# Second attention: each query pair in one weight block with the rope columns twice, keys projected first; the last expert group in smaller pieces with its end on two engines

## The chip, the cores and the metric

One NeuronCore of one Trainium2 chip runs the whole program in one launch. The time is device microseconds of that core, the median over several runs of the same kernel. The kernel before takes 1916.61 us (three runs, 1916.44 to 1920.51). All arithmetic is float32 or its rounded parts, batch 1, 256 tokens (two tiles of 128 partitions), model width 1024.

## What is computed

A small network of two blocks and a third one behind it: FoX attention, SwiGLU, MLA attention (the second attention), SwiGLU, final norm; then a token mixer (stick-breaking attention and gated delta rule), cross attention over 256 memory rows, and PEER, a layer that reads 16 expert rows for each token and each of 8 heads. The parts that matter here:

```python
def rope(x, positions):                       # x1, x2: the halves of 32 columns
    out = concat([x1 * cos - x2 * sin, x1 * sin + x2 * cos])

def mla_attention(xn, positions, k, v, w_dq, cq_norm, w_uq, w_o):   # 16 heads
    c_q = rmsnorm(xn @ w_dq, cq_norm)                     # 768 wide
    q = (c_q @ w_uq).reshape(B, S, 16, 64 + 32)
    q = concat([q[..., :64], rope(q[..., 64:], positions)])
    # k of a head: 64 columns c_kv @ w_uk, and 32 rope columns shared by all heads
    o = causal_block_attention(q, k, v, 1 / sqrt(96))
    return o @ w_o

def peer(xn, w_pq, subkeys, peer_u, peer_v):
    # for each of 8 heads: the 16 best of 16384 experts for each token, and then
    act = gelu(einsum('thkd,td->thk', peer_u[eb], xb)) * gate
    out = einsum('thk,thkd->td', act, peer_v[eb])

# and at the very end: h + out, root-mean-square norm with g_final
```

## The kernel before

Each engine has a program of its own, in order, and they meet at semaphores. `Tally` counts the waits, also in loops. SP issues nearly all loads; weights go into four single slots of SBUF, `SLOT[0..3]`. `fill(s, ...)` waits until slot s is used up and then issues; TensorE frees a slot with `release(s)`, which queues the signal, and `first(m)` hangs it on the next matmul that takes one, so a slot is free when a matmul *behind* its last reader has ended. PSUM has eight banks; `take` and `evacuated` make TensorE wait until VectorE ("v") or ScalarE ("a") has read a bank.

**Second attention.** The 16 heads run as 8 pairs. For a pair TensorE does `mla_proj` (line 853): queries of head 0 and head 1, each 96 rows by 256 columns over six chunks of 128 (slot 0, 576 KB), then the 64 key rows of each head over two chunks (slot 1, 128 KB), each head in a group of its own, then a product of the copied queries `QRAW` with the matrix `rot`, which turns the rope halves. Each matmul of float32 is two passes. ScalarE copies queries and keys out (`mla_copy`, 1544). VectorE's `rotate` (2128) multiplies the turned queries by sines and the queries by cosines, and adds: three operations. The shared rope rows of the keys are computed once and stand in rows 64 to 96 of `KT` for both heads. `mla_scores` (TensorE 874, VectorE 2136) gives the scores with a contraction over 96 rows, ScalarE the exponentials (`two_probs`), and `attend` (654) turns them (`flip`), multiplies them with the values (`mix_values`) and turns the result (`turn`). The order in the loop is scores of pair i+1, projection of pair i+2, attention of pair i+1. SP issues the query fill and then the key fill of a pair (`qk`, 367).

**ffn** (both). Behind the last block VectorE adds the residual in four halves, ScalarE squares each half (1475), VectorE does mean and reciprocal, and ScalarE the square root (`root`, 1399).

**Expert layer.** For each head and token tile ("unit", 16 in all) GpSimd gathers 16 rows of 8 KB a token (u and v, `gather`, 1790) into a ring. VectorE takes the dot product of a row with the token (`dots`, 2559); after four of them ScalarE does Gelu, VectorE the gate weight, ScalarE four diagonal matrices (`diagonals`, 1721), and TensorE multiplies them with the v rows into four PSUM banks that add up over all heads (`mix_v`, 1354), four passes a row. After the last unit of a tile a product with zeros closes its two banks. `finish(t)` (2590) on VectorE adds both banks to `H`, squares each half, sums, takes mean and reciprocal, has ScalarE take the root, and multiplies the whole tile with it and the gain; SP then writes the tile out (469).

## Time and profile before

| | us |
|---|---|
| median of 3 runs | 1916.61 |
| profiled execution | 1915.84 |
| its span | 1913.6 |
| TensorE busy (matmul) | 1693.1 (88%) |
| VectorE busy | 1036.7 (54%) |
| ScalarE busy | 530.0 (28%) |
| GpSimd busy | 348.0 (18%) |
| mean granted TensorE clock | 0.956 of 2.4 GHz |

The profile is of one execution. Its span is the time between the first and the last instruction; 2.2 us of the execution's time lie outside. PE is TensorE, PEld its weight loads, DVE is VectorE, ACT ScalarE, POOL GpSimd, SP SyncE, and SPq the transfers that SP issues. A timeline row names start, length, engine, line of the kernel, operation with what it writes and reads, how many instructions it merges, and in brackets the engine's idle time before it with what ended it. A row "x32" of 7.22 us is 32 passes of TensorE. The second attention's loop stands from about 431 to 534 us, the two ffn end near 370 and 766, the expert layer begins near 1240, and its last unit at about 1875.

### The profile page before, as it was taken

The numbers are of one execution on the slowest core, as the hardware profiler recorded it, in microseconds if no ns is written. First come the engines' busy times: TensorE is split into PE (matmuls) and PEld (weight loads), VectorE is DVE, ScalarE is ACT, GpSimd is POOL, SyncE is SP. The second block draws the span as 40 slices with busy tenths as digits, with TensorE's granted clock in tenths as the row PEclk, the third lists the DMA queues.
The fourth block names the chain that finished last, engine by engine and source line by source line (L and its number), as shares of the span: only waits on it lengthen the run. The fifth ranks groups of instructions, "written<-read, shape, count | busy, mean of one in ns | idle before, by whom it ended". The sixth has DMA issues, their size and how long they took to land.

```text
span 1913.6 us, 22345 instructions
## 1 busy us (share of the span) xinstructions
PE 1693.1 (88%) x7695; PEld 1174.5 (61%) x7695; DVE 1036.7 (54%) x2431; ACT 530.0 (28%) x1067; POOL 348.0 (18%) x296
## 2 busy tenths in 40 slices
PE   6798999889989999799999999987888877888876
PEld 5687999856649999587565586543443433444332
DVE  5454555433435555345735201587676777766764
ACT  2353444312324443243211001122221212212211
POOL 2550000000000000000000000244434444443440
PEclk9899999999999999899999999989999989899988
DMA  7342655501336665143232532299999999999995
GB/s 240 114 111 89 197 173 179 166 16 54 115 91 198 197 179 161 36 136 115 100 121 76 209 133 80 106 419 421 421 422 421 421 421 421 422 420 422 421 421 241
DMA packets 205557, 435.63 MB, mean 228 GB/s; under 512 B 11584, under 2 KB 136896, under 8 KB 171584
## 3 DMA queue, kind: packets, MB, share of 16 engines
q0 software_dynamic: 36864, 268.45, 33.8%
q1 hardware_dynamic: 168640, 166.45, 27.3%
q8 instruction: 36, 0.59, 0.1%
q14 instruction: 17, 0.14, 0.0%
HBM read 433.79 MB, written 1.05 MB: 227 GB/s over the span
## 4 chain that ended last, share of the span: by engine, by line
PE 68%; DMA 20%; DVE 7%; issue 3%; ACT 2%; POOL 1%; SPq 0%; DVEq 0%; POOLq 0%
PE ps L505 36%; DMA OT<-in_peer_uv,IX 17%; PE ps L1359 10%; PE ps L691 6%; PE ps L1149 3%; PE ps L1006 3%; PE ps L1019 3%; PE ps L536 1%; DMA SLOT<-in_fox_w_in 1%; PE ps L511 1%; DVE SLOT L2563 1%; DVE SLOT_R L1927 1%; PE ps L1098 1%; DVE AR L2241 1%; PE ps L595 1%
## 5 line engine op out<-in xcount | busy, mean ns | idle before, releaser
L1797 POOL DMA_INDIRECT SLOT<-in_peer_uv,IX x128 | 138.3, 1080 | 1345.7 <-DVE IX L2557 1097.8
L1359 PE MATMUL ps<-SLOT,AR 128*128 128x512 f32 x512 | 268.0, 680 | 102.4 <-ACT AR L1725 102.4
L1359 PEld LDWEIGHTS ps<-SLOT,AR 128*128 128x128 f32 x512 | 109.6, 219 | 254.5 <-issue 132.2
L505 PE MATMUL ps<-ARH 128*128 128x256 f32 x2112 | 257.0, 283 | 5.1 <-DVE SM L1958 5.1
L505 PEld LDWEIGHTS ps<-ARH 128*128 128x128 f32 x2112 | 256.2, 192 | 7.0 <-issue 5.5
L2563 DVE SCALAR_TENSOR_TENSOR SLOT<-SLOT,V 128x1024 f32<-128x1024 f32 x128 | 153.4, 1224 | 77.7 <-DMA SLOT<-in_peer_uv,IX 75.6
L1927 DVE TENSOR_TENSOR ARH<-SLOT,ARH 128x2048 fp32r<-128x2048 f32 (+1 forms) x88 | 154.1, 1755 | 47.9 <-ACT ARH L1437 31.2
L1359 PE MATMUL ps<-AR 128*128 128x512 f32 x320 | 142.5, 594 | 8.1 <-ACT AR L1725 8.1
L691 PE MATMUL ps<-ARH 128*128 128x512 f32 x528 | 123.9, 390 | 0.0
L1719 ACT ACTIVATE AR<-AR 128x4 f32<-128x4 f32 x64 | 13.1, 205 | 380.9 <-DVE SLOT L2563 180.2
L691 PEld LDWEIGHTS ps<-ARH 128*128 128x128 f32 x528 | 97.7, 188 | 19.4
L1359 PEld LDWEIGHTS ps<-AR 128*128 128x128 f32 x320 | 59.7, 190 | 80.4 <-issue 64.1
L2563 DVE SCALAR_TENSOR_TENSOR AR<-AR,V 128x1024 f32<-128x1024 f32 x80 | 95.3, 1222 | 24.6 <-DMA AR<-in_peer_uv,IX 24.6
L1797 POOL DMA_INDIRECT AR<-in_peer_uv,IX x80 | 91.7, 1146 | 76.3 <-PE ps L1359 70.8
L505 PE MATMUL ps<-XT,SLOT 128*128 128x256 f32 (+1 forms) x464 | 102.1, 380 | 0.8 <-issue 0.8
L505 PEld LDWEIGHTS ps<-XT,SLOT 128*128 128x128 f32 (+1 forms) x464 | 87.2, 189 | 13.9 <-issue 1.5
L505 PE MATMUL ps<-AR,SLOT 128*96 128x256 f32 (+2 forms) x384 | 87.5, 386 | 1.2 <-issue 1.2
L1725 ACT ACTIVATE AR<-CT,AR 128x128 f32<-128x128 f32 x256 | 81.8, 390 | 17.6 <-DVE AR L2577 17.6
L1941 DVE TENSOR_TENSOR AR<-AR,ps 128x256 f32<-128x256 f32 x44 | 18.5, 421 | 125.3 <-ACT AR L1447 125.3
L1437 ACT CAST ARH<-SLOT 128x2048 fp32r<-128x2048 f32 x44 | 83.4, 1899 | 0.0
L505 PEld LDWEIGHTS ps<-AR,SLOT 128*96 128x96 f32 (+2 forms) x384 | 64.4, 170 | 22.6 <-issue 5.1
L505 PE MATMUL ps<-XT 128*128 128x256 f32 (+1 forms) x288 | 60.8, 367 | 6.7 <-DMA XT<-in_w_pq_by_head 5.6
(396 smaller groups left out, 2488.0 us busy)
## 6 DMA issues: line engine op xcount, KB each, us to landing
SLOT<-in_w_gate SPq DMA_DIRECT2D x44, 512.0 KB, 4.0
SLOT<-in_w_up SPq DMA_DIRECT2D x44, 512.0 KB, 5.3
SLOT<-in_w_down SPq DMA_DIRECT2D x44, 512.0 KB, 5.6
SLOT<-in_w_in SPq DMA_DIRECT2D x9, 2048.0 KB, 8.1
SLOT<-in_fox_w_in SPq DMA_DIRECT2D x16, 512.0 KB, 5.3
SLOT<-in_w_ckv SPq DMA_DIRECT2D x4, 2048.0 KB, 8.1
XT<-in_w_pq_by_head SPq DMA_DIRECT2D x8, 1024.0 KB
SLOT<-in_mla_w_uq SPq DMA_DIRECT2D x8, 576.0 KB
```

What stands on the lines that cost most here:

```text
L505: m = pe.matmul(outp, l, r, start=(n_ == 0), stop=(n_ == len(pairs) - 1))
L511: return pe.transpose(outp, src, IDENT)
L691: m = pe.matmul(ps[:, o_, :], l_, r_, start=(start and b == 0 and n_ == 0), stop=(stop and b == 1 and n_ == 2))
L1006: m = pe.matmul(ps[:, b, :], cols(XT, t, k), slot(s_, KC, 512)[:, k, :], start=(k == 0), stop=(k == KC - 1))
L1019: m = pe.matmul(ps[:, b, h * P:(h + 1) * P], l(h), r(h), start=True, stop=True)
L1149: m = pe.matmul(ps[:, b, :], cols(X, t, k), w[:, k, :], start=(k == 0), stop=(k == KC - 1))
L1359: m = pe.matmul(ps[:, 2 * t + c, :], DIAG[:, j, :], v_row(j)[:, c * 512:(c + 1) * 512], start=False, stop=False)
L1437: act.copy(WGU[:, b, 0].rearrange("p g k n -> p (g k n)"), SLOT[b][:, 0:2 * KC * P]).then_inc(sem("high_ready"), 1)
L1725: act.activation(DIAG[:, j, :], IDENT, ACT.Copy, scale=AV[:, t, j:j + 1]).then_inc(sem("diag_ready"), 1)
L1797: pool.indirect_dma_start(PAIR[j], None, pairs, bass.IndirectOffsetOnAxis(IX[:, t, j:j + 1], 0)).then_inc(gathered[j], 16)
L1927: return TT(out_, x, high.bitcast(F32), ALU.subtract)
L2563: m = STT(u_row(j), u_row(j), 1.0, V[:, t, :], ALU.mult, ALU.mult, accum_out=DOT[:, t, j:j + 1])
```

## The change

*Weights, on the host.* `w_uq` is laid out by pair in 256 columns instead of 192: for head 0 64 plain columns, 32 rope columns, the same 32 with halves swapped; for head 1 32 rope, 32 swapped, 64 plain. A row of the new tensor is 2048 values (8192 bytes; before, 1536 values). `w_krope` holds the 32 rope columns four times. Constants: `rot` for 128 rows, frequencies for all rows, a `sign` column.

*Second attention.* The queries come out of the projection as 128 rows a head that already hold both forms; one multiplication by a table `TABQ` (ones, cosines, signed sines) replaces copy, rotation product and the three operations. Scores contract over 128 rows. Keys of both heads come from one group of 128 rows, projected ahead of the queries; ScalarE copies each head's 64 rows. The signal that frees the key slot hangs on the queries, the one that frees the query slot on the next transpose, or, for the first pair, on the first score matmul. SP still issues the query fill first; it is 768 KB now. The table costs VectorE two memsets, two copies and two multiplications where two copies were.

*ffn.* ScalarE does a one-element Sqrt behind its last Silu, ahead of the squares.

*Last unit and end.* The rows of the last unit of tile 1 go in groups of 4, 4, 4, 2, 1, 1. The last row's two matmuls close the banks themselves. The end of tile 1: VectorE adds a half, ScalarE squares the first half and the second half's last 256 columns, VectorE squares the other 256; ScalarE writes the first half of the output from a product with the gain that VectorE made ahead, VectorE the second; each half has a transfer of 256 KB. Tile 0 ends as before, with its two additions ahead of its squares. Several semaphores of the token mixer are merged into two (`heads_ready`, `decays_ready`), signalled and waited for in the same order.

```diff
@@ host
-    arrays["in_w_krope"] = np.concatenate([np.zeros((D, 64), np.float32), np.asarray(inputs["w_kv_a"])[:, KVR:]], 1)
+    arrays["in_w_krope"] = np.ascontiguousarray(np.tile(np.asarray(inputs["w_kv_a"])[:, KVR:], (1, P // ROPE)))
+    by_pair = [nope[:, :, 0], rope[:, :, 0], swapped[:, :, 0], rope[:, :, 1], swapped[:, :, 1], nope[:, :, 1]]
@@ sync
-            qk(rows(w_uq, 0, 192), w_uk[:, :, 0:P])
+            qk(rows(w_uq, 0, 2 * P), w_uk[:, :, 0:P])
             with T.loop("mla", PAIRS - 1) as i:
-                qk(dyn(w_uq, i * 192 + 192, 192), w_uk[:, :, ds(i * P + P, P)])
+                qk(dyn(w_uq, i * 2 * P + 2 * P, 2 * P), w_uk[:, :, ds(i * P + P, P)])
...
+            sp.wait_ge(sem("result"), 2)
+            sp.dma_start(y[:, 1, 0:512], H[:, 1, 0:512]).then_inc(sem("out_done"), 16)
+            sp.wait_ge(sem("last_result"), 1)
+            sp.dma_start(y[:, 1, 512:], H[:, 1, 512:]).then_inc(sem("out_done"), 16)
@@ tensor
             def mla_proj():
+                pe.wait_ge(here[1], T.next(here[1], 16))
+                take(6)
+                group(ps[:, 6, 0:S], ((slot(1, 2, P)[:, k, :], CKT[:, k, :]) for k in range(2))).then_inc(full["a"][6], 1)
+                release(1)
+                T.add(free["a"][6])
                 pe.wait_ge(here[0], T.next(here[0], 16))
                 take(0)
                 for hh in range(2):
-                    m = group(ps[0:96, 0, hh * S:(hh + 1) * S], ((slot(0, 6, 192)[:, k, 96 * hh:96 * hh + 96], CQT[:, k, :]) for k in range(6)))
+                    m = group(ps[:, 0, hh * S:(hh + 1) * S], ((slot(0, 6, 2 * P)[:, k, P * hh:P * hh + P], CQT[:, k, :]) for k in range(6)))
                 release(0)
...
-                for hh in range(2):
-                    m = group(ps[0:64, 6, hh * S:(hh + 1) * S], ((slot(1, 2, P)[:, k, 64 * hh:64 * hh + 64], CKT[:, k, :]) for k in range(2)))
-                release(1)
...
-                first(pe.matmul(ps[0:96, 7, 0:S], const("rot", 96), QRAW[0:96, 0, :], start=True, stop=True))
-                pe.matmul(ps[0:96, 7, S:2 * S], const("rot", 96), QRAW[0:96, 1, :], start=True, stop=True).then_inc(full["v"][7], 1)
...
             def mla_scores(i):
-                evacuated(6, 7)
+                evacuated(0, 6)
                 for hh in range(2):
                     take(1 + hh)
-                    pe.matmul(ps[:, 1 + hh, 0:P], QT[0:96, hh, 0:P], KT[0:96, hh, 0:P], start=True, stop=True)
+                    first(pe.matmul(ps[:, 1 + hh, 0:P], QT[:, hh, 0:P], KT[:, hh, 0:P], start=True, stop=True))
...
+            mix_v(1, range(TOPK - 1))
+            mix_v(1, range(TOPK - 1, TOPK), closing=True)
@@ scalar, ffn
                 for b in range(2):
                     gated(b)
+                act.activation(ASCR[:, 0:1], CT[:, 0:1], ACT.Sqrt)
@@ scalar, mla_copy
-                act.wait_ge(full["a"][0], T.next(full["a"][0]))
-                act.copy(QRAW[0:96, :, :], view(ps[0:96, 0, :], 2, S)).then_inc(free["a"][0], 1)
                 act.wait_ge(full["a"][6], T.next(full["a"][6]))
-                act.copy(KT[0:64, :, :], view(ps[0:64, 6, :], 2, S)).then_inc(free["a"][6], 1)
+                act.copy(KT[0:64, 0, :], ps[0:64, 6, 0:S])
+                act.copy(KT[64:P, 1, :], ps[64:P, 6, 0:S]).then_inc(free["a"][6], 1)
@@ scalar, end
-            weigh(1, between=lambda: root_of(0))
-            root_of(1)
+            weigh(1, between=lambda: root_of(0), groups=LAST)
+            act.activation(ASCR[:, 0:1], CT[:, 0:1], ACT.Sqrt)
+            for c, part in ((0, slice(0, 512)), (1, slice(256, 512))):
+                act.wait_ge(sem("grown"), T.next(sem("grown")))
+                m = act.activation(square(1, c)[:, part], H[:, 1, c * 512:(c + 1) * 512][:, part], ACT.Square, accum_out=SS[:, 2 * c:2 * c + 1])
+            m.then_inc(sem("squared"), 1)
...
+            act.activation(H[:, 1, 0:512], V[:, 0, 0:512], ACT.Copy, scale=RS[:, 1:2]).then_inc(sem("result"), 1)
@@ vector
             def rotate():
-                dve.wait_ge(full["v"][7], T.next(full["v"][7]))
-                TT(ANG[R96, 0:2, :], view(ps[R96, 7, :], 2, S), SIN[R96, :, :], ALU.mult)
-                TT(ANG[R96, 2:4, :], QRAW[R96, :, :], COS[R96, :, :], ALU.mult).then_inc(chain, 1)
-                dve.wait_ge(chain, T.next(chain))
-                TT(QT[R96, :, :], ANG[R96, 0:2, :], ANG[R96, 2:4, :], ALU.add).then_inc(free["v"][7], 1)
-                T.add(free["v"][7])
+                dve.wait_ge(full["v"][0], T.next(full["v"][0]))
+                TT(QT[:], view(ps[:, 0, :], 2, S), TABQ, ALU.mult).then_inc(free["v"][0], 1)
+                T.add(free["v"][0])
...
+            def finish_last():
+                half = grown_half(1, 0)
+                signal("grown")
+                TT(V[:, 0, 0:512], half, ROWG[:, 0:512], ALU.mult).then_inc(sem("gained_half"), 1)
+                half = grown_half(1, 1)
+                signal("grown")
+                STT(square(1, 1)[:, 0:256], half[:, 0:256], 1.0, half[:, 0:256], ALU.mult, ALU.mult, accum_out=SS[:, 1:2]).then_inc(chain, 1)
+                dve.wait_ge(chain, T.next(chain))
+                dve.wait_ge(sem("squared"), T.next(sem("squared")))
+                dve.tensor_reduce(SS[:, 3:4], SS[:, 0:3], AX, ALU.add).then_inc(chain, 1)
...
+                STT(half, half, RS[:, 1:2], ROWG[:, 512:], ALU.mult, ALU.mult).then_inc(sem("last_result"), 1)
```

## Rows read from the trace of the kernel before

**Rows 1.** The page's part 4, the chain that ended last, by engine.
```profile
PE 68%; DMA 20%; DVE 7%; issue 3%; ACT 2%; POOL 1%; SPq 0%; DVEq 0%; POOLq 0%
```

**Rows 2.** Timeline, one head pair: start us, us, engine, line, operation, idle before.
```profile
469.60 7.22 PE L505 MATMUL ps<-AR,SLOT 128*96 128x256 f32 x32
...
474.98 0.58 ACT L1546 COPY AR<-ps 96x512 f32<-96x512 f32 x1 [2.38 <-PE ps L505]
...
475.73 0.37 SPq L355 DMA_DIRECT2D SLOT<-in_mla_w_uq  x1
...
476.74 0.67 PE L870 MATMUL ps<-AR,CT 96*96 96x256 f32 x2
...
477.68 0.82 PE L511 MATMUL ps<-CT,AR 128*128 128x128 f32 x6
...
477.70 0.37 SPq L355 DMA_DIRECT2D SLOT<-in_w_uk  x1
...
479.16 0.88 PE L505 MATMUL ps<-V,AR 128*128 x6 [0.66 <-ACT AR L1423]
...
481.07 0.46 PE L878 MATMUL ps<-AR 96*128 96x128 f32 x2 [0.19 <-issue]
...
482.45 7.22 PE L505 MATMUL ps<-AR,SLOT 128*96 128x256 f32 x32
```

**Rows 3.** DMA: a quarter us (last column GB/s); w_uk's landing; issues, median to landing.
```profile
478.25:478.50 0.25, 0.25 (x3) 0.01 (x1) 0.25 (x2) 0.25 (x1) 0.00 (x0) 1.00 1.08 369
...
DMA to landing us min/median/max: 2.1/2.7/4.2
...
SLOT<-in_w_up SPq DMA_DIRECT2D x44, 512.0 KB, 5.3
...
SLOT<-in_w_in SPq DMA_DIRECT2D x9, 2048.0 KB, 8.1
...
SLOT<-in_w_ckv SPq DMA_DIRECT2D x4, 2048.0 KB, 8.1
```

**Rows 4.** Timeline, TensorE: first, second and last projection block of the loop.
```profile
431.04 7.26 PE L505 MATMUL ps<-AR,SLOT 128*96 128x256 f32 x32 [1.24 <-issue]
...
441.59 0.46 PE L878 MATMUL ps<-AR 96*128 96x128 f32 x2 [2.25 <-issue]
...
442.97 8.90 PE L505 MATMUL ps<-AR,SLOT 128*96 128x256 f32 x32
...
520.89 7.21 PE L505 MATMUL ps<-AR,SLOT 128*96 128x256 f32 x32
```

**Rows 5.** Stretch in the second block: busy PE, PEld, DVE, ACT, POOL; PEclk; DMA.
```profile
444.00:446.00 2.00, 2.00 (x6) 1.29 (x6) 0.93 (x3) 1.79 (x8) 0.00 (x0) 0.50 0.00 0
```

**Rows 6.** Timeline, VectorE after the angle tables.
```profile
391.20 0.42 DVE L1835 SCALAR_TENSOR_TENSOR XS<-AR 128x256 f32<-128x256 f32 x1 [3.25 <-ACT ASCR L1397]
```

**Rows 7.** Timeline, behind the first ffn.
```profile
370.77 1.28 ACT L1402 ACT_TABLE_LOAD   x1
...
371.18 0.17 DVE L1819 RECIPROCAL RS<-RS 128x2 f32<-128x2 f32 x1
```

**Rows 8.** Timeline of the last 25 us; then the last output transfer's landing.
```profile
1890.51 1.88 PE L1359 MATMUL ps<-SLOT,AR 128*128 128x512 f32 x4
...
1891.77 1.22 DVE L2563 SCALAR_TENSOR_TENSOR SLOT<-SLOT,V 128x1024 f32<-128x1024 f32 x1 [1.25 <-DMA SLOT<-in_peer_uv,IX]
...
1894.23 1.23 DVE L2563 SCALAR_TENSOR_TENSOR OT<-OT,V 128x1024 f32<-128x1024 f32 x1 [1.23 <-DMA OT<-in_peer_uv,IX]
...
1896.38 7.11 PE L1359 MATMUL ps<-SLOT,AR 128*128 128x512 f32 x12 [3.99 <-ACT AR L1725]
...
1905.66 0.69 DVE L2597 TENSOR_TENSOR H<-H,ps 128x512 f32<-128x512 f32 x1 [9.77 <-PE ps L1383]
...
1909.26 1.28 DVE L2611 SCALAR_TENSOR_TENSOR H<-H,RS,ROWG 128x1024 f32<-128x1024 f32 x1 [0.27 <-ACT RS L1704]
...
out<-H SPq DMA_DIRECT2D x1, 512.0 KB, 2.6
```

More of the change, by code:

```diff
@@ L306, in hd, with square @@
             return X[:, t, h * P:(h + 1) * P]
+        FOURS = [range(4 * g, 4 * g + 4) for g in range(4)]
+        LAST = FOURS[:3] + [range(12, 14), range(14, 15), range(15, 16)]
         def u_row(j):
             return PAIR[j][:, 0:D]
+        def square(t, c):
+            return XT[:, 4 * t + 2 * c:4 * t + 2 * c + 2, :].rearrange("p a b -> p (a b)")
         def v_row(j):
@@ L815, in _ @@
             take(4)
-            group(ps[0:96, 4, 0:S], ((WPAD[:, k, :], XT2[:, k, :]) for k in range(KC))).then_inc(full["a"][4], 1)
+            group(ps[:, 4, 0:S], ((WPAD[:, k, :], XT2[:, k, :]) for k in range(KC))).then_inc(full["a"][4], 1)
             T.add(free["a"][4])
@@ L838, in _ @@
             take(5)
-            pe.matmul(ps[0:96, 5, 0:S], const("rot", 96), KRT[0:96, :], start=True, stop=True).then_inc(full["v"][5], 1)
+            pe.matmul(ps[:, 5, 0:S], const("rot"), KRT, start=True, stop=True).then_inc(full["v"][5], 1)
             T.add(free["v"][5])
@@ L1352, in match, with mix_v @@
                 release(1)
-            def mix_v(t, g):
-                for j in range(4 * g, 4 * g + 4):
+            def mix_v(t, places, closing=False):
+                for j in places:
                     pe.wait_ge(sem("diag_ready"), T.next(sem("diag_ready")))
                     for c in range(2):
-                        m = pe.matmul(ps[:, 2 * t + c, :], DIAG[:, j, :], v_row(j)[:, c * 512:(c + 1) * 512], start=False, stop=False)
+                        b = 2 * t + c
+                        m = pe.matmul(ps[:, b, :], DIAG[:, j, :], v_row(j)[:, c * 512:(c + 1) * 512], start=False, stop=closing)
                         if c == 0:
                             first(m)
-                    m.then_inc(ring_used[j], 1)
+                        if closing:
+                            m.then_inc(full["v"][b], 1)
+                            T.add(free["v"][b])
+                    if not closing:
+                        m.then_inc(ring_used[j], 1)
             take(0, 1, 2, 3)
@@ L2557, in route, with dots @@
                 dve.tensor_copy(IX[:, t, :], PAF[:, t, :]).then_inc(sem("expert_ready"), 1)
-            def dots(t, g):
-                for j in range(4 * g, 4 * g + 4):
+            def dots(t, places):
+                for j in places:
                     dve.wait_ge(gathered[j], T.next(gathered[j], 16))
@@ L2582, in unit, with grown_half @@
+            def unit(t, between=None, groups=FOURS):
+                dots(t, groups[0])
                 gates(t)
[L2583 to L2586 removed]
+                weigh(t, groups[0])
+                for g, places in enumerate(groups[1:], 1):
+                    dots(t, places)
+                    weigh(t, places)
                     if g == 1 and between:
                         between()
[L2590 to L2600 removed]
+            def grown_half(t, c):
+                b = 2 * t + c
+                half = H[:, t, c * 512:(c + 1) * 512]
+                dve.wait_ge(full["v"][b], T.next(full["v"][b]))
+                TT(half, half, ps[:, b, :], ALU.add).then_inc(free["v"][b], 1)
+                T.add(free["v"][b])
+                settled(b)
+                return half
@@ new lines, in root_from, with finish_first @@
+            def root_from(t, total):
+                TS(RS[:, t:t + 1], total, 1.0 / D, EPS, ALU.mult, ALU.add).then_inc(chain, 1)
+                dve.wait_ge(chain, T.next(chain))
+                dve.reciprocal(RS[:, t:t + 1], RS[:, t:t + 1]).then_inc(sem("rms_ready"), 1)
+            def finish_first():
+                halves_ = [grown_half(0, c) for c in range(2)]
+                for c, half in enumerate(halves_):
+                    m = STT(square(0, c), half, 1.0, half, ALU.mult, ALU.mult, accum_out=SS[:, 4 + c:5 + c])
@@ L2628, in _ @@
             unit(0)
-            unit(1, between=lambda: finish(0))
-            finish(1)
+            unit(1, between=finish_first, groups=LAST)
+            finish_last()
 PER_ITER = {
```

213 lines of the change are left out of this document (102 added, 111 removed).

## The prediction

> **What bounds the kernel now.** I first read the page's chain, which shows the engine that ended each stretch last. TensorE holds two thirds of it [rows 1]. The rest is mostly row gathers of the peer stage, which this change leaves as they are. What counts is therefore how long TensorE takes in the second attention, and what stands behind the last gathered row. For the first I read the timeline of one head pair; for the second, the timeline of the last 25 us. A change smaller than 0.2% (3.8 us) could not be told from none here.
>
> In the pair loop TensorE starts a projection block at 469.60 and the next at 482.45: a period of 12.85 us [rows 2]. The block is 24 passes for the queries and 8 for the keys, 7.22 us, so 0.22 us a pass. The queries end at about 474.8, where ScalarE starts their copy. The four rotation passes stand at 476.74, the transposes at 477.68, and the next scores at 481.07. TensorE hardly rests, so the loop is bound by TensorE. The weights sit in single slots. The query slot is refilled only once its last matmul has been followed by another (issue at 475.73), the key slot at 477.70, and both fills are needed at 482.45. Today the query fill has 6.7 us of cover.
>
> **The change, part by part.**
>
> *Rotation and keys.* Both heads' keys now come out of one group of 4 passes instead of two of 4, and the rotation's 4 passes go. Between the end of the queries and the transposes lie 2.86 us today [rows 2]; in the new order about 0.1 us of it is left, and the keys ahead of the queries cost 4 x 0.22 + 0.1 = 0.97 us. TensorE's own period would be 12.85 - 2.86 + 0.1 + 0.97 = 11.07 us, 1.78 us less. Wider operands (128 rows and columns instead of 96) cost nothing: a pass is as long as its 256 columns. VectorE does one 512-wide multiply (0.69 us, as the add in [rows 8]) where it did three operations, done near 7.1 us of the period while scores start near 9.7. ScalarE's two key copies run behind its exponentials, about 3 us into the period, when it used to idle (2.38 us before the query copy). Neither is on the path.
>
> *The fills.* SP issues the query fill first, then the key fill, while TensorE now wants the keys first. Freeing the query slot also moves: the matmul that follows the queries is now the first transpose, so it stands behind the whole block. With T the start of a block, the queries end at T + 0.97 + 5.23 = T + 6.2, the transpose ends at T + 6.45, and SP follows some 0.5 us later (from the first rotation matmul's end, about 477.2, to the key fill at 477.70), at T + 6.94. The key fill is issued 0.4 us after it. Together they bring 896 KB instead of 704. How long until the keys are there is not in the trace; bounds come from near rows. Today the key fill lands 2.7 us after its own issue, 4.7 after the query fill's [rows 3]. Issued at once it would save about 0.4, hence a floor of 4.2 even if the extra 192 KB cost nothing in 1 KB pieces. A ceiling is the ffn's pair w_gate and w_up, 1024 KB in 512-byte pieces: the second lands 5.3 us after its own issue, 5.7 after the first's, less 128 KB at the plateau's 0.369 MB per us, 0.4 us: 5.3. I take 4.75, nearest to today's own row: 4.7 - 0.4, plus 0.197 MB at the 0.369 MB per us of the plateau, 0.5. Then keys can start at T + 6.94 + 4.75 + 0.15 = T + 11.84. That is later than 11.07: the loop turns from TensorE-bound into fill-bound, and of 1.78 us a pair only 1.0 is kept.
>
> *First and last pair.* Pair 0 starts at 431.04 [rows 4]. Its queries end near 437.2, the multiply near 438.1, scores start near 438.3 instead of 441.59. But its query slot is freed by the first score matmul, so the fill is issued at 439.0 and the second block starts at 443.9, not 442.97: the early scores gain nothing and 0.9 us is lost. The second block took 8.90 us instead of 7.22, with the granted clock at 0.50 (1.2 GHz) after TensorE's rest of 2.25 us [rows 5]; I keep these 1.68 us, since the rest gets longer. Third block: 443.9 + 6.94 + 1.68 + 4.9 = 457.4. Five more periods of 11.84: the last block at 516.6, where it stood at 520.89, and the last one is 1.78 shorter: 4.3 + 1.8 = 6.1 us gained. With the floor of 4.2 the period is 11.3 and the gain 9.9; with a ceiling of 5.3 it is 12.4 and the gain 2.2.
>
> *Preparation.* After its angles VectorE gets six small table operations for two, four more of 256 columns or less; at no more than 0.42 us each, as the product in [rows 6], 1.7 us. It then waits 3.25 us for the latents [rows 6], which hides them; without that cover they would cost up to 1.7. The wider krope and position loads stand 15 us and more ahead of use. Merged semaphores keep signals and waits in the same order: nothing.
>
> *Early Sqrt.* Behind each ffn ScalarE loads its table at 370.77 for 1.28 us, until 372.05, while VectorE's reciprocal, started at 371.18, is done at 371.35 [rows 7]. With the table loaded while TensorE finishes the block, the root starts near 371.55: 0.5 us, twice, 1.0 us. Floor 0, should Square want another table than Sqrt's; then the load merely moves. The Trainium skill, "ScalarE: Activation LUTs", section "What ACT_TABLE_LOAD costs", adds a drain of about 1.38 us to each switch. By it this part would be worth up to 3.8 us; the trace has nothing between load and root, so it stands at 1.0.
>
> *The tail.* The last row lands at 1894.23; its product, ScalarE's and VectorE's small steps take 2.15 us until TensorE starts at 1896.38, with all four rows of the group [rows 8]: 16 passes. Twelve of them took 7.11 us where at full clock they take 5.3 (four in 1.88 with the drain of the last, so 0.43 a pass), as TensorE had rested 3.99 us. VectorE starts at 1905.66. Rows land 2.5 us apart (products at 1891.77 and 1894.23). New: rows 12 and 13, whose products end some 5 us before row 15's, are ready at 1891.4 and run from 1892.2 (end of the group before) to 1895.6, row 14 to 1897.3, row 15 (ready 1896.4) c=0 to 1898.1 and c=1 to 1899.0, with no rest and so no half clock. VectorE starts near 1898.4: add 0.7, signal 0.17, gain multiply 0.7, add 0.7, signal 0.17 (each as the reciprocal of [rows 7]), 256-wide square 0.5 [rows 6], then 1.0 for five short steps of 0.2 (the wait for ScalarE's squares, sum, mean, reciprocal, root), near 1902.4, and 0.7 for the half multiply, beside ScalarE's half: 1903.1, against 1910.54 (1909.26 and 1.28). Two output transfers of half size, the second issued 0.4 us behind, end about as long after that as the one of 512 KB today (2.6 us): 7.2 us gained. If half clock for one spell comes back, 1.7 less: 5.5 to 7.5. Gather traffic isn't touched, so nothing earlier in that stage moves.
>
> *Sum.* 6.1 + 1.0 + 7.2 = 14.3. The profiled execution took 1915.84 (span 1913.6 and 2.2 around it), 0.8 under the median of 1916.61: 1901.5 in its frame, 1902.3 in the median's. I say 1902.
>
> **Rivals.**
> A. The fills land in time (4.75 is too long by 0.8 or more), the period is TensorE's 11.07 from the third block on. 443.35 + 12.4 + 5 x 11.07 = 511.1, gain 9.8 + 1.8 = 11.6; total 19.8, 1896.8. For it: larger pieces; a floor of 4.2 comes near. Against: today's 704 KB already take 4.7. Chance 0.2.
> B. The new rest of 0.8 us in each period drops the clock, as 2.25 us did [rows 4, 5]. Six blocks at 1.7 us more: the loop loses 4 instead of gaining 6; total gain 4 to 6, about 1911 to 1913. Against: today's rest of 0.66 us ahead of the value matmuls [rows 2] doesn't show in the length of the blocks, 7.22 us in each. Chance 0.1.
> C. Slower: the new weight tensor has a row pitch of 8192 bytes where it was 6144, and its reads run at half rate. 0.79 MB at 0.19 per us makes 7.4 us to landing: blocks at 446.5, 462.6, then every 14.5, the last at 535.2: 12.5 lost, 8.2 gained elsewhere, 1921. It decides from a landing of about 6.3 us. Against it: w_ckv with the same pitch of 8192 lands in 8.1 us like w_in with 22 KB [rows 3]. Chance 0.02. The page "DMA: Bandwidth & Descriptors" of the Trainium skill, section on latency and other measured facts, tells of such a loss for power-of-two pitches, from 512 KiB up; by it nothing would happen at 8 KB, and the w_ckv row agrees.
> D. The change does not do what it says: Square or the halved keys bring table loads or waits I don't see, leaving only the tail, 1909. Chance 0.06.
> The forecast itself: 0.62; its own range is 1898 to 1909.
>
> **How the numbers follow.** Most likely 1902. The sum's lower bounds (2.2 + 0 + 5.5) give 1909, and A gives 1897: 1897 to 1909 leaves out B, C and a little more, under 2 in 10. Faster by over 0.2% (under 1912.8): the forecast, A, D and half of B, 0.93. Same: the other half of B, 0.05. Slower: C, 0.02.
>
> **What would show it.** The period of the loop 11.8 and, before each key group, TensorE idle 0.7 us for the transfer of w_uk; 11.1 and no such wait is A. Granted clock 0.5 in each period is B. Landing of w_uk 4.3 after its issue; over 6 is C. A second block later than 443. Sqrt's load at 363, the root near 371.5. TensorE without rest from 1885 to 1899, and 7 us between the last multiply now and then. The prediction is wrong if the fills aren't what the key group waits for, or if TensorE's clock falls in the last unit.

## The result, and the profile after

| | before | after |
|---|---|---|
| median, first comparison | 1916.53 us (6 runs) | 1909.23 us (6 runs, 1904.17 to 1910.09) |
| ratio, 95% interval | | 0.995 [0.9939, 0.996] |
| median, second comparison (control, below) | 1919.54 us (11 runs) | 1905.99 us (6 runs, 1900.43 to 1912.55) |
| ratio, 95% interval | | 0.9935 [0.9916, 0.9954] |
| profiled execution, its span | 1915.84, 1913.6 | 1910.02, 1907.8 |
| mean granted TensorE clock | 0.956 | 0.953 |

The change makes the kernel faster, by 7.3 us in the first comparison and 13.6 in the second, and neither interval holds 1. Part of the difference between the two lies in the kernel before: its own median goes from 1916.53 to 1919.54 in the sets of runs used here. The twelve runs of the changed kernel have a median of 1908.0. The forecast of 1902 lies 7.2 below the first median, which is just above its range of 1897 to 1909, and 4.0 below the second, which is inside.

Lines of the page after: the chain by engine (as [rows 1]), and from the groups of instructions TensorE's blocks of the pair loop and the transfers behind them (busy us, mean ns, idle before them and what ended most of it).

```profile
PE 69%; DMA 16%; DVE 10%; issue 3%; ACT 1%; POOL 1%; SPq 1%; another core or an unknown queue 1%; DVEq 0%; ACTq 0%
...
L517 PE MATMUL ps<-AR,SLOT 128*128 128x256 f32 x352 | 81.4, 392 | 12.5 <-DMA SLOT<-in_w_uk 11.3
...
SLOT<-in_w_uq_by_pair SPq DMA_DIRECT2D x8, 768.0 KB
```

The second line is new: TensorE's blocks now wait 11.3 us for the transfer of `w_uk`. One head pair shows how, in the timeline (as [rows 2]):

```profile
463.70 6.31 PE L517 MATMUL ps<-AR,SLOT 128*128 128x256 f32 x28 [1.67 <-DMA SLOT<-in_w_uk]
...
469.85 0.82 PE L523 MATMUL ps<-CT,AR 128*128 128x128 f32 x6
470.34 0.37 SPq L364 DMA_DIRECT2D SLOT<-in_w_uq_by_pair  x1
...
471.09 0.37 SPq L364 DMA_DIRECT2D SLOT<-in_w_uk  x1
471.22 0.88 PE L517 MATMUL ps<-V,AR 128*128 x6 [0.55 <-ACT AR L1434]
...
473.04 0.46 PE L883 MATMUL ps<-AR 128*128 128x128 f32 x2
...
475.49 6.31 PE L517 MATMUL ps<-AR,SLOT 128*128 128x256 f32 x28 [0.90 <-DMA SLOT<-in_w_uk]
```

and the chain that ended last, in order of time, through the same pair:

```profile
463.70 6.31 PE ps L517 x28
470.01 0.12 PE ps L523
...
470.34 0.37 SPq L364
...
471.09 4.35 DMA SLOT<-in_w_uk
475.44 0.04 issue
475.49 6.31 PE ps L517 x28
```

The loop goes block, first transpose, query fill issued, key fill issued, key fill landed, block. Vector and scalar work do not occur in it. The period is 475.49 - 463.70 = 11.79 us, where it was 12.85; the four periods after it last 11.69 to 11.95. The first blocks and the last one (as [rows 4]):

```profile
435.47 6.28 PE L517 MATMUL ps<-AR,SLOT 128*128 128x256 f32 x28 [1.24 <-issue]
442.54 0.49 PE L883 MATMUL ps<-AR 128*128 128x128 f32 x2 [0.78 <-DVE AR L2154]
...
448.86 9.33 PE L517 MATMUL ps<-AR,SLOT 128*128 128x256 f32 x28 [4.74 <-DMA SLOT<-in_w_uk]
...
522.71 6.31 PE L517 MATMUL ps<-AR,SLOT 128*128 128x256 f32 x28 [1.13 <-DMA SLOT<-in_w_uk]
```

Behind the first ffn (as [rows 7]) the Sqrt table is loaded at 365.45, and the root follows the reciprocal at once:

```profile
365.45 1.28 ACT L1483 ACT_TABLE_LOAD   x1
...
373.66 0.20 ACT L1413 ACTIVATE RS<-RS 128x2 f32<-128x2 f32 x1 [0.63 <-DVE RS L1840]
```

The end (as [rows 8]): TensorE does not rest, VectorE starts 1.06 us after the last row's first pass, and both halves are written from 1903.9.

```profile
1892.24 7.03 PE L1365 MATMUL ps<-SLOT,AR 128*128 128x512 f32 x16
...
1895.94 1.22 DVE L2584 SCALAR_TENSOR_TENSOR OT<-OT,V 128x1024 f32<-128x1024 f32 x1 [0.81 <-DMA OT<-in_peer_uv,IX]
...
1898.06 1.28 ACT L1764 ACT_TABLE_LOAD   x1
...
1899.10 1.88 PE L1365 MATMUL ps<-OT,AR 128*128 128x512 f32 x4
...
1900.16 0.69 DVE L2617 TENSOR_TENSOR H<-H,ps 128x512 f32<-128x512 f32 x1 [2.56 <-PE ps L1365]
...
1903.88 0.75 DVE L2656 SCALAR_TENSOR_TENSOR H<-H,RS,ROWG 128x512 f32<-128x512 f32 x1 [0.27 <-ACT RS L1770]
1903.94 0.72 ACT L1773 ACTIVATE H<-V,RS 128x512 f32<-128x512 f32 x1
1904.68 0.34 SPq L481 DMA_DIRECT2D out<-H  x1
1905.07 0.43 SPq L483 DMA_DIRECT2D out<-H  x1
```

**The span cut into stages.** To see where the gain is and where it is lost again, I cut each profiled execution at the same instructions: the first pass of the latents' projections, the first block of the pair loop, the first output pass behind it, the start of the second ffn's last down group, the next transposes, the last row's product, the end. Each stage is a difference of two starts in the timeline.

```
us                  before  after   after again
start to projections 380.02  381.70   379.11
to the first block    51.02   53.77    53.77
pair loop            102.33   97.68    96.16
to second ffn's end  224.89  227.55   226.18
behind it             15.90   15.21    15.21
to last product     1120.07 1120.03  1119.34
tail                  19.37   11.86    11.83
span                 1913.6  1907.8   1901.6
```

Three stages are shorter (loop, behind the ffn, tail: 4.65 + 0.69 + 7.51), and one is longer by 2.75 in both executions: the preparation, which the prediction costed at nothing. The first stage (which holds the first ffn's 0.66) and the fourth differ between two executions of the same changed kernel by 2.6 and 1.4 us. That is the clock: in the record it falls to 0.50 in 32 stretches of the span before and in 33 after, each of which costs 1.7 us or two or three times as much (84.3 and 88.9 us in all), and which of them occur differs from one execution to the next. In the second comparison the changed kernel's runs go from 1900.43, at a mean clock of 0.957, to 1912.55, at 0.952. In the fourth stage, for example, 1.7 us of clock are lost before, 5.1 after and 3.4 in the second execution. So two sets of runs are compared below by stages first, and by medians second.

### The profile page after: what moved, and what is told of

The parts are those of the page before. It is cut to its first block, busy times and chain, and to the rows that moved or that the text cites. A ratio compares the mean times of both kernels' runs of the same rounds, so it can differ in the third digit from the quotient of the medians.

```text
span 1907.8 us, 22177 instructions
## 1 busy us (share of the span) xinstructions
PE 1684.8 (88%) x7627; PEld 1178.1 (62%) x7627; DVE 1028.2 (54%) x2422; ACT 528.9 (28%) x1077; POOL 348.5 (18%) x296
## 4 chain that ended last, share of the span: by engine, by line
PE 69%; DMA 16%; DVE 10%; issue 3%; ACT 1%; POOL 1%; SPq 1%; another core or an unknown queue 1%; DVEq 0%; ACTq 0%
PE ps L517 36%; PE ps L1365 13%; DMA OT<-in_peer_uv,IX 11%; PE ps L703 6%; PE ps L1154 3%; PE ps L1011 3%; PE ps L1024 3%; DVE SLOT L2584 2%; PE ps L548 2%; DMA SLOT<-in_w_uk 2%; DMA SLOT<-in_peer_uv,IX 2%; DMA SLOT<-in_fox_w_in 1%; PE ps L523 1%; DVE SLOT_R L1948 1%; PE ps L1103 1%
## 5 line engine op out<-in xcount | busy, mean ns | idle before, releaser
L1731 ACT ACTIVATE AR<-AR 128x4 f32<-128x4 f32 (+1 forms) x66 | 13.5, 205 | 373.8 <-DVE SLOT L2584 187.9
L517 PE MATMUL ps<-XT,SLOT 128*128 128x256 f32 x464 | 102.1, 380 | 0.8 <-issue 0.8
L517 PEld LDWEIGHTS ps<-XT,SLOT 128*128 128x128 f32 x464 | 87.6, 190 | 13.5 <-issue 1.5
L517 PE MATMUL ps<-AR,SLOT 128*128 128x256 f32 x352 | 81.4, 392 | 12.5 <-DMA SLOT<-in_w_uk 11.3
L517 PEld LDWEIGHTS ps<-AR,SLOT 128*128 128x128 f32 x352 | 68.3, 196 | 25.5 <-DMA SLOT<-in_w_uk 14.1
```

What stands on the lines that cost most here:

```text
L517: m = pe.matmul(outp, l, r, start=(n_ == 0), stop=(n_ == len(pairs) - 1))
```

## The experiments

All are the changed kernel with one edit, unless said otherwise. Every one computes the whole result.

**One part alone.** The second attention as before, the rest changed:

```diff
-            TT(QT[:], view(ps[:, 0, :], 2, S), TABQ, ALU.mult).then_inc(free["v"][0], 1)
+            TT(ANG[R96, 0:2, :], view(ps[R96, 7, :], 2, S), SIN[R96, :, :], ALU.mult)
+            TT(ANG[R96, 2:4, :], QRAW[R96, :, :], COS[R96, :, :], ALU.mult).then_inc(chain, 1)
+            ... (with layout, projection, copies and scores as before)
```

> The changed kernel with its second attention (weights' layout, order, rotation, key copies) put back to the old form; the new end of the last unit and the early Sqrt stay. Theory: the new attention is worth 4.6 us (what its loop shows between its first projection block and the output projection in the trace of after), so this runs 4.6 us longer than the 1909.2 of the changed kernel: 1913.5 to 1915, and its tail is as short as in after (11.9 us from the last row's product to the end). Rival: the attention part gives nothing on balance, because the clock of TensorE falls more often around it, and the 7.3 us are the tail alone; then this is at 1908 to 1910.

Measured: 1910.85 us (12 runs, 1907.15 to 1916.55), 0.9964 [0.9951, 0.9977] of before. Stages: preparation 50.91, loop 102.15, both within 0.2 us of before. It took the preparation's 2.75 us back and gave up the loop's gain. The time lies between what the theory (1913.5 to 1915) and the rival (1908 to 1910) gave, and the theory had left out the preparation. By the two stages together the new attention is worth 1.6 us in the first execution of the changed kernel and 3.1 in the second; by means it is worth 3.0 (1911.1 against 1908.1, the first six runs) or 4.0 (against 1907.1, all twelve).

The last groups and the end as before, the rest changed:

```diff
-            weigh(1, between=lambda: root_of(0), groups=LAST)
+            weigh(1, between=lambda: root_of(0))
+            root_of(1)
```

> The changed kernel with the end of the last unit put back (groups of 4, closing with zeros, one engine, one output transfer); the new attention and the early Sqrt stay. Theory: the tail is worth 7.5 us (19.4 us from the last row's product to the end of the span before, 11.9 after), so 1916 to 1917; what is left, attention and Sqrt, is then nearly nothing against before in spite of 4.6 and 1.4 us in the traces. Rival: attention and Sqrt give their 6 us and the tail less, because the last row lands earlier or the clock stays up: 1911 to 1913.

Measured: 1914.93 us (12 runs, 1908.23 to 1921.12), 0.9984 [0.9969, 1.0]. Tail 19.41, preparation 53.67, loop 95.72. The time again lies between theory and rival. By means the changed tail is worth 7.0 us (1915.1 against 1908.1) or 8.0 (against 1907.1), by its stage 7.5.

**Is the loop bound by the order of the two fills?** SP issues the key fill first, as TensorE uses it first:

```diff
-            qk(rows(w_uq, 0, 2 * P), w_uk[:, :, 0:P])
+            def keys_then_queries(q_src, k_src):
+                fill(1, (slot(1, k_src.shape[1], k_src.shape[2]), k_src))
+                fill(0, (slot(0, q_src.shape[1], q_src.shape[2]), q_src))
```

> The changed kernel with one thing turned round: SP issues the key fill of a pair before the query fill, as TensorE wants them. Theory (the loop is bound by the fills: period 11.8 us, of which TensorE waits 0.7 to 1.7 us for w_uk): keys no longer wait, the query fill lands in time, the period falls to 11.1 us and the wait for w_uk is gone; 4 to 5 us less than the changed kernel, about 1905. Rival (the period comes from something else, and the wait for w_uk only stands in for it): period stays at 11.8, time 1909.

Measured: 1898.72 us (6 runs, 1889.78 to 1899.45), 0.9888 [0.9867, 0.9908]. Loop 87.78 instead of 97.68 (96.16 in the second execution). That is about twice the 4 to 5 us expected. Its timeline:

```profile
470.48 6.21 PE L521 MATMUL ps<-AR,SLOT 128*128 128x256 f32 x28
472.14 0.37 SPq L364 DMA_DIRECT2D SLOT<-in_w_uk  x1
...
476.52 0.82 PE L527 MATMUL ps<-CT,AR 128*128 128x128 f32 x6
477.09 0.37 SPq L364 DMA_DIRECT2D SLOT<-in_w_uq_by_pair  x1
...
479.64 0.46 PE L887 MATMUL ps<-AR 128*128 128x128 f32 x2
...
481.02 3.23 PE L521 MATMUL ps<-AR,SLOT 128*128 128x256 f32 x14
```

The key fill now goes out at 472.14, 1.66 us into the block, long before it is needed, and the query fill has the time of the key passes besides. From here on no fill holds up a block: the query fill lands just as the key passes end. The period is 481.02 - 470.48 = 10.54 us (10.55 to 10.59 the next times). It is TensorE's own, with its wait of 0.55 us for ScalarE's copy of the turned probabilities in it. The order of two lines on SP cost the changed kernel 1.24 us in each period. Of the loop's 9.90 us, 4.80 stand from the fourth block on and 5.10 before it, where the key fills go out earlier as well (the first at 1.74 us into the block instead of 8.86). What is left is one wait of 3.3 us in front of the second block's queries, as the waits of TensorE in the loop show (us in total, times, longest):

```profile
PE ps L521 <- DMA SLOT<-in_w_uq_by_pair: 3.7, 2, 3.3
```

The other way to match the two orders: SP's as it is, and TensorE projects the queries before the keys.

```diff
+            (in mla_proj: the six chunks of both heads' queries, release(0), and then)
                 pe.wait_ge(here[1], T.next(here[1], 16))
                 take(6)
                 group(ps[:, 6, 0:S], ...).then_inc(full["a"][6], 1)
                 release(1)
```

> The changed kernel with the queries projected ahead of the keys again (new layout and one key group kept). Theory: the query slot is freed 0.9 us earlier in a period and 2 us earlier for the first pair, both fills land before they are wanted, the period is TensorE's own 11.1 us, the second block starts near 446 less the shift instead of 4.7 us after the scores; 6 us less than the changed kernel, about 1903. Rival: no change, 1909, if the period isn't made by the fills.

Measured: 1900.84 us (6 runs, 1894.28 to 1902.15), 0.9901 [0.9884, 0.9919]. Loop 91.18, period 481.47 - 470.49 = 10.98 us. From the fourth block on the fills are in time; but ScalarE's two key copies now stand between the block and its copy of the turned probabilities, and TensorE's wait for that is 0.99 us in each period where it was 0.55. That is the 0.44 that the period is longer than with the key fill first. The next three periods last 12.16, 11.54 and 11.95 us, though, as the granted clock falls twice in this part of the loop, where it is 1.00 with the key fill first:

```profile
478.34 0.88 PE L517 MATMUL ps<-V,AR 128*128 x6 [0.99 <-ACT AR L1434]
...
491.00:495.00 4.00, 3.93 (x13) 3.35 (x13) 3.19 (x12) 0.99 (x4) 0.00 (x0) 0.57 0.24 79
...
515.00:519.00 4.00, 4.00 (x14) 3.33 (x14) 3.18 (x12) 1.32 (x6) 0.00 (x0) 0.57 1.01 361
```

In this stretch no wait of TensorE is longer than 0.99 us. So from the fourth block to the loop's end this order takes 5.28 us more than the key fill first (58.14 against 52.86), some 3 of them by the clock, and before it 1.88 less. Whether the longer wait brings the clock down was not tested on its own; the profile is of one execution.

**The tail's two parts.** Rows in groups of four as before, the split end kept:

```diff
-        LAST = FOURS[:3] + [range(12, 14), range(14, 15), range(15, 16)]
+        LAST = FOURS
```

> The changed kernel, but with the last unit's rows in groups of four as before; the end stays split over two engines. It tells the two parts of the tail's gain (7.5 us together) apart. From the last row's product to the end of the span the kernel before took 19.37 us and the changed one 11.86. The theory: the smaller groups keep 12 of 16 passes of TensorE from standing behind the last row (9.3 us of passes then, 1.9 now) and save the rest before them with its half clock, so they carry most of it: 19.37 less the split end alone (some 1.5 us) gives about 17.5 us here. Rival: the split end carries most, then about 14 us here.

Measured: 1913.21 us (one run), tail 17.82. Its timeline:

```profile
1893.18 1.22 DVE L2584 SCALAR_TENSOR_TENSOR OT<-OT,V 128x1024 f32<-128x1024 f32 x1 [1.23 <-DMA OT<-in_peer_uv,IX]
...
1895.33 7.11 PE L1365 MATMUL ps<-SLOT,AR 128*128 128x512 f32 x12 [3.98 <-ACT AR L1737]
...
1903.34 0.69 DVE L2617 TENSOR_TENSOR H<-H,ps 128x512 f32<-128x512 f32 x1 [8.50 <-PE ps L1365]
```

The rest of 3.98 us and the slow twelve passes of [rows 8] are back. Of the tail's 7.51 us the groups carry 17.82 - 11.86 = 5.96 and the split end 19.37 - 17.82 = 1.55.

**The early Sqrt.** Taken out again:

```diff
-                act.activation(ASCR[:, 0:1], CT[:, 0:1], ACT.Sqrt)
```

> The changed kernel without the early one-element root behind each ffn. The theory: the table load is paid again behind the squares, and the time from the end of each ffn's last block to TensorE's next work goes back from 9.43 and 8.89 us to about 10.1 and 9.6, 1.4 us in all. Rival: the difference of 1.36 us was something else of the change; then the two stretches stay at 9.4 and 8.9.

Measured: 1913.83 us (one run). From the last down group to the next transposes 10.28 us in the first ffn and 15.90 in the second, where the changed kernel has 9.60 and 15.21: 0.68 and 0.69 us, 1.37 in all. ScalarE in this kernel:

```profile
373.53 1.28 ACT L1413 ACT_TABLE_LOAD   x1
374.82 0.20 ACT L1413 ACTIVATE RS<-RS 128x2 f32<-128x2 f32 x1
```

**Why the preparation got longer.** In it TensorE rests ahead of the projection of the values. The rest, in brackets, and the length of the 16 passes behind it, in the kernel before and the changed one:

```profile
414.40 7.13 PE L505 MATMUL ps<-SLOT,AR 128*128 128x512 f32 x16 [1.84 <-DVE AR L1861]
```

```profile
416.22 8.83 PE L517 MATMUL ps<-SLOT,AR 128*128 128x512 f32 x16 [1.95 <-DVE AR L1882]
```

The granted clock (second last but two) in the ten microseconds with these passes, of before and of after:

```profile
414.00:424.00 10.00, 7.13 (x16) 2.96 (x16) 4.91 (x10) 1.71 (x5) 0.00 (x0) 1.00 0.00 0
```

```profile
416.00:426.00 10.00, 8.83 (x16) 3.55 (x16) 3.21 (x7) 1.71 (x5) 0.00 (x0) 0.83 0.01 2
```

TensorE waits for VectorE, which copies the shared rope rows and then scales the latents. In the changed kernel the two copies write 64 rows each, and run one behind the other (414.79 and 415.09); before, the second started 0.21 us after the first. That is the 0.11 us that the rest is longer. Behind it the clock falls to the lower of its two levels (1.2 GHz) for a spell that costs 1.70 us, and the 24 transposes that follow take 5.49 us instead of 4.57. (The 4.57 hold half clock too; with none they take 2.94, in the last but one experiment.) 0.11 + 1.70 + 0.92 = 2.73 of the 2.75. To test it from both sides, first a shorter rest in the changed kernel: the latents scaled before the copies.

```diff
+            gained(CKT, "ckv", 2)
             dve.tensor_copy(KT[64:P, 0, :], KRT[64:P, :])
             dve.tensor_copy(KT[0:64, 1, :], KRT[0:64, :]).then_inc(chain, 1)
             dve.wait_ge(chain, T.next(chain))
             signal("krope_ready")
-            gained(CKT, "ckv", 2)
```

> The changed kernel, with VectorE scaling the key and value latents before it copies the shared rope rows, so that TensorE rests for about 1.3 us instead of 1.95 ahead of the value projection. The theory (the rest of 1.95 us lets the granted clock fall): the value projection takes 7.15 us instead of 8.85, and from the projections' first pass to the first block of the pair loop it is about 50.5 us instead of 53.77. Rival (the clock falls for another reason, for instance by the load pattern before it): it stays at 8.85 and only the 0.6 us of rest are gained, 53.1.

Measured: 1907.15 us (one run), and

```profile
419.01 7.13 PE L517 MATMUL ps<-SLOT,AR 128*128 128x512 f32 x16 [1.27 <-DVE AR L1882]
```

with a preparation of 49.98 us, 3.79 less. Then a longer rest in the kernel before, by one idle copy on VectorE:

```diff
             dve.wait_ge(chain, T.next(chain))
+            dve.tensor_copy(ANG[R96, 3, :], KRT[R96, :]).then_inc(chain, 1)
+            dve.wait_ge(chain, T.next(chain))
```

> The kernel before with one more small copy on VectorE ahead of the latents' scaling, so that TensorE's rest of 1.84 us ahead of the value projection becomes about 2.1. The theory that the length of this rest decides the clock: the value projection takes 8.85 us instead of 7.15 and the way to the pair loop 53 us instead of 51.0. Rival (the length of the rest does not decide): 7.15 and 51.3.

Measured: 1918.3 us (one run; the kernel before had 1919.3 beside it), and

```profile
413.96 8.83 PE L505 MATMUL ps<-SLOT,AR 128*128 128x512 f32 x16 [2.17 <-DVE AR L1861]
```

with a preparation of 53.84 us, 2.82 more than before. In this stage the old attention pays the same price once its rest is lengthened, so it is not the new tables or the wider matmuls. In the whole it hardly pays: the second block of the loop, 8.90 us in the kernel before [rows 4], ran at full clock here, behind the same rest of 2.25 us ahead of the scores,

```profile
445.04 7.22 PE L505 MATMUL ps<-AR,SLOT 128*96 128x256 f32 x32
```

and the loop took 100.46 us instead of 102.33. So a spell added in one place can be missing in the next. In the changed kernel the loop didn't give the price back: 97.68 and 96.16 us with the long rest, 96.11 with the short one. Over all fourteen profiled executions (those below counted): rests of 1.27 (four) and 1.84 (two) left the passes at 7.13 us, rests of 1.95 to 2.17 (eight) had them at 8.83.

**Both repairs together.** Key fill first and latents scaled first:

> The changed kernel with both findings: SP issues the key fill ahead of the query fill, and VectorE scales the latents before it copies the shared rope rows. The theory (both act on stretches of their own, so they add): period 10.55 us and the value projection at 7.15 us; against the kernel with the key fill alone (1898.7) it gains what the shorter rest gains, 3.8 us from the projections' first pass to the first block, about 1895, with the count of other half-clock spells of 1.7 us each as spread. Rival (a spell avoided here comes up a little later, as TensorE's clock has to fall somewhere): the stretch up to the first block is 3.8 us shorter, but the whole gains under 2 us, 1897 to 1899.

Measured: 1891.95 us (6 runs, 1886.31 to 1899.81), 0.9869 [0.9843, 0.9895]. Preparation 50.03, loop 88.09: each stage as in its own experiment. By means it is 3.8 us under the key fill alone (1892.9 against 1896.7), which is what the shorter rest gives in its stage. But the six runs of either kernel spread over 10 and 13 us, so the times alone don't exclude the rival (under 2 us in the whole).

**The first pair turned round as well.** TensorE projects pair 0's queries before its keys, and SP loads queries first for pairs 0 and 1:

```diff
+            qk(rows(w_uq, 0, 2 * P), w_uk[:, :, 0:P])
+            qk(rows(w_uq, 2 * P, 4 * P), w_uk[:, :, P:2 * P])
+            with T.loop("mla", PAIRS - 2) as i:
+                keys_then_queries(dyn(w_uq, i * 2 * P + 4 * P, 2 * P), w_uk[:, :, ds(i * P + 2 * P, P)])
...
-            mla_proj()
+            mla_proj(first_pair=True)
```

> The kernel with the key fill first and the earlier scaling, and in the first pair alone the queries ahead of the keys, with the fills for the first two pairs also queries first. The theory: in the key-first order the second block of the loop waits some 3.3 us for its queries, as the first pair's query slot is freed only by the first scores; with the queries first in pair 0 the key projection frees the slot a block's part earlier, about 2 us off, so about 1893. Rival: the second block then waits for its keys instead, which are issued second; nothing gained, 1895, or 1 us lost for the key copies that now stand ahead of the scores.

Measured: 1890.33 us (4 runs, 1889.2 to 1893.92), 0.986 [0.9841, 0.9879]: the fastest version, with a loop of 84.89 us, 3.2 less. Its timeline:

```profile
431.41 6.28 PE L522 MATMUL ps<-AR,SLOT 128*128 128x256 f32 x28 [1.15 <-issue]
...
437.29 0.37 SPq L364 DMA_DIRECT2D SLOT<-in_w_uq_by_pair  x1
...
438.87 0.46 PE L898 MATMUL ps<-AR 128*128 128x128 f32 x2 [1.18 <-ACT AR L1574]
...
442.41 6.31 PE L522 MATMUL ps<-AR,SLOT 128*128 128x256 f32 x28 [2.00 <-DMA SLOT<-in_w_uk]
```

The query fill goes out 5.88 us into the block instead of 7.78 in the changed kernel (8.17 with the key fill first), and the second block starts after 11.00 instead of 13.39 us; it does wait for its keys, as the rival said, but for 2.00 us, not 4.74, and no half clock follows. By means the whole is 2.0 us faster than without (1890.9 against 1892.9), which four and six runs hardly settle; in the profiled execution half clock stood in the tail (13.29 us instead of 11.83).

**The scaling alone, timed.**

> The changed kernel with the earlier scaling of the latents alone, timed. The theory: 3.8 us less than the changed kernel's 1909.2 between the projections and the pair loop, 1905.5. Rival (the avoided half clock is given back by spells elsewhere): 1907 to 1909.

Measured: 1899.39 us (4 runs, 1896.53 to 1903.62), 0.9897 [0.9877, 0.9917]; preparation 48.75, loop 96.92. That is 9.8 us under the changed kernel's first median, while its stage explains 3.8 to 5.0. It is under the theory's 1905.5 as well as the rival's 1907 to 1909. Hence a control:

> The changed kernel once more, unaltered, as a control for the others: the kernel with the latents scaled earlier came out 9.8 us under the changed kernel's first median (1899.39 against 1909.23), where its own stretch explains 3.8. If the first median of the changed kernel stands for it, this gives 1908 to 1910 and the other 6 us come from half-clock spells elsewhere in so few runs; if the runs of one call differ among themselves by that much, it gives 1903 to 1906, and a difference between two calls is worth only what the traces account for.

Measured: 1905.99 us (6 runs, 1900.43 to 1912.55), 0.9935 [0.9916, 0.9954]. Between the two cases, nearer to the second: the runs of one kernel differ by 12 us, and six of them do not fix its median to better than some 3 us. Against the mean of both sets (1907.1) the scaling alone stands at 7.4 less (1899.7) in four runs; 3.8 to 5.0 of it is seen in its stage, and its profiled execution shows no cause for the rest (85.6 us of lost clock, between the 88.9 and 83.7 of the changed kernel's two). Over all runs the mean clock does differ, 0.958 in these four against 0.955 in the twelve of the changed kernel. By an estimate (0.003 of 1900 us) that is some 6 us, the spells of the stage included. Whether the edit does that or the few runs, stays open.

## Why the prediction was right or wrong

*The loop turns from TensorE-bound to fill-bound: the mechanism right, the 0.05 us by luck.* The period was forecast at 11.84 and is 11.79. Its terms were off against each other. The query fill is issued at T + 6.64, not 6.94: the first transpose ends at T + 6.43, as forecast (6.45), but SP follows 0.21 us later and not 0.5. SP needs 0.75 us between the two issues, not 0.4. The key fill lands 4.35 us after its own issue (4.24 to 4.50 in the next periods), which is the 4.75 - 0.4 of the forecast; that was a value chosen between 4.2 and 5.3.

*TensorE's own period: wrong by 0.5.* I gave 11.07; the key fill first shows 10.54. From the block's start to the transposes it takes 6.04 us where it took 8.08 [rows 2]: 2.04 less, where I had counted 1.79 (the sum gives 11.06, not 11.07) by adding two gaps of 0.1 and rounding the pass up. From the transposes to the scores it is 3.12 instead of 3.39, as TensorE's waits of 0.66 and 0.19 ahead of the value matmuls and the scores [rows 2] shrank to 0.55 and nothing; that I had kept. It didn't touch the forecast, since the fills set the period, but it hid what stood to be had: the fill-bound loop kept 1.06 of 2.31 us a pair.

*First pair: the mechanism right, the size too small.* The early scores gain nothing. The query fill went out at T0 + 7.78 (forecast 7.96), but the key fill 1.08 us behind it, so the second block started at T0 + 13.39 and not 12.86. Behind a rest of 4.74 us the clock then fell for 3.0 us of lost time instead of 1.68 in the first execution, and the third block came 1.3 us late (14.84 against 13.5). In the second the block took 7.71 us instead of 9.33 and the third came after 13.33. So the loop gained 4.65 us in one and 6.17 in the other; forecast 6.1.

*Preparation: the step that failed.* I costed it at nothing, on the ground that a wait for the latents hides the table operations. It does: the wait went from 3.25 to 1.67 us. But the two copies of the rope rows stand behind that wait, between it and the scaling that TensorE waits for, and I didn't look at them: they went from 32 to 64 rows. The delay itself is 0.11 us. The price is 2.75, since TensorE's rest of 1.84 us became one of 1.95 and the clock fell behind it; the two experiments with a shorter and a longer rest show that this is the cause of the longer stage. No run lengthened the rest from 1.84 to 1.95 alone. The rule that I had used in the tail and in the first pair (a longer rest may cost a spell at half clock) I didn't apply to a rest that the change lengthens by a tenth of a microsecond.

*Early Sqrt: right in place, under by 0.37.* 0.68 and 0.69 us instead of twice 0.5: the root now follows the reciprocal at once, where I had left a gap ahead of it. The trace again has nothing between table load and root, 373.53 + 1.28 = 374.81 and 374.82. By the Trainium skill, "ScalarE: Activation LUTs", "What ACT_TABLE_LOAD costs", the part would have been worth up to 3.8 us, an estimate with its drain of about 1.38 us for each switch; it was worth 1.37, so here the measurement speaks against the added drain.

*Tail: right, to 0.3.* Forecast 7.2, measured 7.51. Counted from the last row's product VectorE starts after 4.22 us (forecast 4.17) and the last multiply ends after 8.72 (forecast 8.87). The lower value that I gave, should half clock come back for one spell, occurred too: the tail is 13.2 to 13.5 us long in three of the other profiled executions, and 14.9 in a fourth.

*The sum.* Forecast 14.3. In the second execution the stages give 6.17 + 0.69 + 7.54 and the first ffn's 0.66, less 2.75, less another 0.3 that is left over in the first, fourth and sixth stage: 12.0, or 1901.6 of span against 1913.6. In the first, 4.65 + 1.35 + 7.51 - 2.75, less 5.0 in the first and the fourth stage, where spells of half clock stand that the execution before didn't have: 5.8. So 1902 would hold for a kernel without the lengthened rest and with no more lost clock elsewhere than before; with that rest 1905 is what the same sum gives, and the two medians lie 4 and 1 above it. How much of that is the spells, these few runs don't settle.

*The rivals.* A (fills in time, 1897) was not the case: 0.88 to 1.13 us of wait stand ahead of each of the last five blocks. B was not: the granted clock from 464 to 524 us is 1.00 with a rest in each period. It wasn't idle, though: with the queries projected first the clock did fall twice in the loop, without a wait longer than 0.99 us.

```profile
464.00:524.00 60.00, 52.15 (x286) 44.20 (x285) 20.16 (x70) 19.69 (x68) 0.00 (x0) 1.00 0.29 89
```

C (slow reads from the wider row pitch) needed a landing 6.3 us after the first issue, and it came 5.10 after it (0.75 + 4.35); its own 7.4 us doesn't follow from its terms, as 0.79 MB at 0.19 instead of 0.369 MB per us adds 2.0 to the 4.75. D was not: the loop did gain, by 3.0 to 4.0 us net of the preparation in the means of the runs.

## What to carry to other kernels

When the order in which an engine uses two loads is turned, turn the order in which they are issued too, and look at which instruction frees each slot: here that was worth about 10 us, as much as the whole change. Ask of every edit ahead of TensorE not only by how much it lengthens a rest, but what the clock does behind it; two copies that came 0.11 us later cost their stage 2.75. And before a few microseconds are read out of two medians, cut both traces into stages at the same instructions and count the stretches at half clock.

## What the runs showed of the hardware

The length of a rest alone does not tell whether TensorE's clock falls. Ahead of the values projection rests up to 1.84 us left it at the upper level (six executions) and rests from 1.95 us on did not (eight), without an exception; but 2.00 us ahead of the second block left the block at 6.31 us, the full speed of its passes, the same rest of 4.7 us cost 1.4 us in one execution of the changed kernel and 3.0 in another, and the same rest of 2.25 us ahead of the scores went with a second block of 8.90 us in the kernel before and of 7.22 in the one with the idle copy. With the queries projected first the clock fell twice in a stretch whose longest wait was 0.99 us. What else decides was not settled. An execution has 26 to 37 such stretches, and 70 to 97 us are lost in them. A mean clock of 0.957 in the fastest run of the control and 0.952 in the slowest makes, by an estimate (0.005 of 1900 us), 9.5 of the 12 us between the two.

Two loads issued one behind the other by SP, of 768 and 128 KB, take 0.75 us between their issues and 5.0 to 5.3 us from the first issue to the second's landing, in every period of the loop from the third block on.
